# A transformer block and two differential-attention layers on one core: operand stacks assembled by DMA, fp32 value products in latent attention, and two squared sums moved into the gated output projection

## The reference

```python
s = jnp.einsum('bqhcd,bkhcd->bhcqk', qb, k) * scale
p = jax.nn.softmax(s, axis=-1)
a = p[:, :, 0] - lam_f * p[:, :, 1]
o = jnp.einsum('bhqk,bkhd->bqhd', a, vf)
```

## Time and profile before

| | us |
|---|---|
| median of 3 runs | 3114.75 (3114.37 to 3115.37) |
| the profiled execution, its own time | 3113.21 |
| its span in the profile | 3111.4 |
| TensorE matmul busy | 2752.8 (88%) |
| TensorE weight load busy | 2348.3 (75%) |
| VectorE busy | 1334.4 (43%) |
| ScalarE busy | 1004.3 (32%) |
| GpSimd busy | 526.2 (17%) |
| mean granted TensorE clock | 0.945 |
| DMA queue 1, share of 16 engines | 16.2% |

### The profile page before, as it was taken

One profiled execution on the slowest core, in us unless ns is written; L12 is line 12 of the kernel. 1 busy time (PEld: TensorE's weight loads), 2 busy tenths in 40 slices (PEclk: granted clock), 3 DMA queues, 4 the chain that ended last, 5 costly groups with the idle time before them and its releaser, 6 DMA issues. The chain is left out here.

```text
span 3111.4 us, 35654 instructions
## 1 busy us (share of the span) xinstructions
PE 2752.8 (88%) x14623; PEld 2348.3 (75%) x14623; DVE 1334.4 (43%) x1631; ACT 1004.3 (32%) x1538; POOL 526.2 (17%) x317
## 2 busy tenths in 40 slices
PE   4999677888879999999975999979997999978999
PEld 1877565787758888888855999768887998767877
DVE  4742753444453333333346212257743412227762
ACT  3312332544242111112213222157631322227640
POOL 0100121331000000000000000048720100008840
PEclk9999888999989999999987999989989999998989
DMA  5531001000211111111102123100022113210022
GB/s 210 176 122 46 14 7 48 14 1 1 95 39 42 49 53 47 47 47 47 48 28 82 50 63 92 48 8 1 1 96 85 68 38 82 52 44 1 1 82 81
DMA packets 58479, 167.92 MB, mean 54 GB/s; under 512 B 6368, under 2 KB 25184, under 8 KB 56672
## 3 DMA queue, kind: packets, MB, share of 16 engines
q1 hardware_dynamic: 58336, 165.92, 16.2%
HBM read 148.93 MB, written 16.97 MB: 53 GB/s over the span
## 5 line engine op out<-in xcount | busy, mean ns | idle before, releaser
L1810 DVE TENSOR_REDUCE da_negmax<-ps 128x1 f32<-128x1040 f32 x136 | 168.4, 1239 | 83.7 <-PE ps L1678 83.6
L1678 PE MATMUL ps<-st_k,st_q 128*128 128x264 f32 (+1 forms) x816 | 173.1, 352 | 35.0 <-DVE st_q L1919 26.5
L1709 PE MATMUL ps<-da_aT,v 128*128 128x128 f32 (+1 forms) x1224 | 161.0, 277 | 32.0 <-DVE da_aT L1736 27.3
L1709 PEld LDWEIGHTS ps<-da_aT,v 128*128 128x128 f32 x1224 | 146.9, 191 | 44.8 <-DVE da_aT L1736 34.9
L2141 DVE SCALAR_TENSOR_TENSOR res<-ps,gates,res 128x1024 f32<-128x1024 f32 x64 | 79.2, 1280 | 226.2 <-PE ps L2190 226.2
L1794 POOL TENSOR_TENSOR da_E<-da_E,da_F 128x1040 f32<-128x1040 f32 x68 | 163.9, 2411 | 5.7
L1678 PEld LDWEIGHTS ps<-st_k,st_q 128*128 128x128 f32 x816 | 125.4, 203 | 46.3 <-issue 27.4
L2104 ACT ACTIVATE ff_wh<-ff_raw 128x1024 fp32r<-128x1024 f32 x64 | 67.5, 1057 | 284.1 <-PE ps L2190 278.4
L2190 PE MATMUL ps<-ff_h_hi,ff_wh 128*128 128x512 f32 x512 | 157.8, 389 | 0.0
L2190 PE MATMUL ps<-ff_h_lo,ff_wh 128*128 128x512 f32 x512 | 157.7, 389 | 0.0
L2190 PE MATMUL ps<-ff_h_hi,ff_wl 128*128 128x512 f32 x512 | 157.7, 389 | 0.0
(11 more groups left out here) (433 smaller groups left out, 6464.6 us busy)
## 6 DMA issues: line engine op xcount, KB each, us to landing
ff_raw<-w_ff SPq DMA_DIRECT2D x64, 512.0 KB, 3.2
ada_w<-w_ada SPq DMA_DIRECT2D x16, 1024.0 KB, 7.5
wo_ring<-w_out SPq DMA_DIRECT2D x22, 512.0 KB, 4.3
residual_spill<-res SPq DMA_DIRECT2D x2, 4160.0 KB, 11.2
res<-xT SPq DMA_DIRECT2D x2, 4096.0 KB, 13.6
ada_w<-w_ada SPq DMA_DIRECT2D x4, 2048.0 KB, 26.8
pqk_raw<-w_in SPq DMA_DIRECT2D x16, 512.0 KB, 3.7
pg_raw<-w_in SPq DMA_DIRECT2D x16, 512.0 KB, 4.1
```

Source lines behind the costliest of these rows:

```text
L1678: mm = pe.matmul(k.ps[:, 3 * (n % 2) + b, a:a + w], q[:, qa:qa + P], kk[:, key:key + w], start=(j == 0), stop=(j == 1))
L1709: mm = pe.matmul(k.ps[:, 7, 0:w], v(g // NQ, t), aT[g % 2][:, t, 0:w], start=(t == 0), stop=(t == NT - 1))
L1810: dve.tensor_reduce(nm[:, n % 4:n % 4 + 1], window(n), AX.X, ALU.max, negate=True).then_inc(s_nm, 1)
```

## The change

Three parts, in neutral words.

1. `Stacks` is rewritten. ScalarE rounds the whole 128-partition key and query of a head (two copies), VectorE or GpSimd subtracts them in place (two subtractions, into the memory of `qk`), and eight DMAs of 64 partitions x 1040 issued from SP put the halves where they belong. The second pass of a component takes the query's rest straight from that memory, a contraction over 64 rows, so that lo·lo is no longer summed. For the first head this is done as the `side` of the value projection; for the others beside the head before, in blocks 0 to 2. The last query block of a head uses only its real rows as weights. `diff_attention`'s SP also loads the first weights of the output projection.
2. Latent attention gets its own function, `latent_heads`: values and transposed weights stay fp32, each batch of transposes is copied once (0 and 2 on ScalarE, 1 on VectorE), value products are one fp32 matmul of 128 columns per key tile and block, and three of the five score passes come ahead of the transposes of two blocks before, two behind.
3. In `GateTiles` the sums of heads 2 and 3 move from before the first product to steps 0 and 1; the turns move from steps 1 and 2 to 3 and 4, the spreads from step 3 on to step 5 on; the order of ScalarE's and VectorE's work around them changes with that.

The core of the diff (classes that only gain a base class with empty methods are left out, as is the removed `attention`):

```diff
-                    for t in key_tiles:
-                        vh, vl = v(g // NQ, t)
-                        for i, (a, b) in enumerate(((vh, ah), (vl, ah), (vh, al))):
-                            mm = pe.matmul(k.ps[:, 7, 0:w], a, b[:, t, 0:w], start=(t == 0 and i == 0), stop=(t == NT - 1 and i == 2))
...
+def latent_heads(nc, k, name, heads, NQ, splits, n_keys, v, scale, o_dst, e0, at0, then, then_at):
...
+    LAG, EARLY = 2, 3
...
+                def pv(g):
+                    pe.wait_ge(s_at1, g + 1)
+                    pe.wait_ge(s_at, 2 * g + 1)
+                    for t in range(NT):
+                        if t == 8:
+                            pe.wait_ge(s_at, 2 * g + 2)
+                        mm = pe.matmul(k.ps[:, 7, 0:P], v(g // NQ, t), aT[g % 2][:, t, :], start=(t == 0), stop=(t == NT - 1))
+                    mm.then_inc(s_pv, 1)
+
+                for g in range(NG + LAG):
+                    i = g - LAG
+                    if g < NG:
+                        scores(g, True)
+                    if i >= 0:
+                        turn(i, 0)
+                        turn(i, 1)
+                    if g < NG:
+                        scores(g, False)
+                    if i >= 0:
+                        turn(i, 2)
+                        pv(i)
...
+                for g in range(NG + LAG + 1):
+                    i = g - LAG
+                    if i >= 1:
+                        out(i - 1)
+                    if 0 <= i < NG:
+                        evacuate(act, i, 0, s_at)
+                    if 1 <= g <= NG:
+                        exps(g - 1)
+                    if 0 <= i < NG:
+                        evacuate(act, i, 2, s_at)
...
+class Stacks(Side):
+    banks = 8
+    PIECES = 8
...
+    def act(self, act, m):
+        if m in (3, 4):
+            self.round(act, 0, m - 3)
+    def dve(self, dve, m):
+        if m in (4, 5):
+            self.rest(dve, 0, m - 4)
+    def sp_last(self, sp):
+        self.copy(sp, 0)
+        sp.wait_ge(self.s_built, 16 * self.PIECES)
+    def round(self, act, h, x):
+        if h > self.head:
+            act.wait_ge(self.s_built, 16 * self.PIECES * (h - self.head))
+        src, dst = ((self.qk[:, AH + h, :], self.kh), (self.qk[:, h, :], self.qh))[x]
+        act.activation(dst[:], src, ACT.Copy).then_inc(self.s_hi, 1)
+    def copy(self, sp, h):
+        half = [slice(0, 64), slice(64, P)]
+        kk, q, low = self.k[h % 2], self.q[h % 2], self.low[:, AH + h, :]
+        if h >= 2:
+            sp.wait_ge(self.s_scores, (h - 1) * self.per_head)
+        done = 2 * (h - self.head)
+        sp.wait_ge(self.s_hi, done + 1)
+        for c in range(2):
+            sp.dma_start(kk[c][half[c], :].bitcast(F32), self.kh[half[c], :].bitcast(F32)).then_inc(self.s_built, 16)
+        sp.wait_ge(self.s_low, done + 1)
+        for c in range(2):
+            sp.dma_start(kk[c][half[1 - c], :].bitcast(F32), low[half[c], :].bitcast(F32)).then_inc(self.s_built, 16)
+        sp.wait_ge(self.s_hi, done + 2)
+        for c in range(2):
+            for r in range(2):
+                sp.dma_start(q[c][half[r], 0:L2].bitcast(F32), self.qh[half[c], :].bitcast(F32)).then_inc(self.s_built, 16)
+        sp.wait_ge(self.s_low, done + 2)
+    def passes(self, h, c, qa, w):
+        half = slice(64 * c, 64 * c + 64)
+        kk = self.k[h % 2][c]
+        return [(self.q[h % 2][c][:, qa:qa + w], kk), (self.low[half, h, qa:qa + w], kk[half, :])]
...
-                        if g // NQ + 1 < heads:
-                            for x in stacks.ACT_TURNS.get(g % NQ, ()):
-                                stacks.round(act, g // NQ + 1, x)
+                        if g // NQ + 1 < heads and g % NQ < 2:
+                            stacks.round(act, g // NQ + 1, g % NQ)
...
-                    if g // NQ + 1 < heads and g % NQ < stacks.REST_STEPS:
-                        if g:
-                            pool.wait_ge(s_A, g)
-                        stacks.rest(pool, g // NQ + 1, g % NQ)
-                        pool.wait_ge(stacks.s_rest, stacks.REST_STEPS * (g // NQ + 1) + g % NQ + 1)
+                    if g // NQ + 1 < heads and 1 <= g % NQ <= 2:
+                        stacks.rest(pool, g // NQ + 1, g % NQ - 1)
...
-        self.at_step = {1: [("turn", 0), ("turn", 1)], 2: [("turn", 2)] if len(self.batches) > 2 else []}
+        self.at_step = {0: [("sum", 2)], 1: [("sum", 3)], 3: [("turn", 0), ("turn", 1)], 4: [("turn", 2)] if len(self.batches) > 2 else []}
         for u in range(U):
-            self.at_step.setdefault(3 + u // 2, []).append(("spread", u))
+            self.at_step.setdefault(5 + u // 2, []).append(("spread", u))
...
     def ahead_pe(self, pe):
+        self.sum_of(pe, 0)
+        self.sum_of(pe, 1)
```

More of the change, by code:

```diff
@@ L254, in _, with open, sp_first, sp @@
                 ada.gains(dve, (0, 1))
-class AdaRest:
+class Side:
+    banks = 5
+    def open(self, freed=None):
+        pass
+    def sp_first(self, sp):
+        pass
+    def sp(self, sp, m):
+        pass
+    def sp_last(self, sp):
+        pass
+    def act(self, act, m):
+        pass
+    def dve(self, dve, m):
+        pass
+    def pe(self, pe, m, j=0):
+        pass
+    def pool(self, pool):
+        pass
+class AdaRest(Side):
     COLS, SLOTS = 256, 3
@@ L993, in gemm_tokens @@
         n_w = len(groups) * KT
-        NBK = 5 if side else 8
+        NBK = side.banks if side else 8
+        few = NBK < 8
         if side:
@@ L1010, in _ @@
                     fetch_first(sp, k, then)
+                if side:
+                    side.sp_last(sp)
             def evac(act, g):
@@ L1042, in _ @@
                        .then_inc(w_lo, 1)
-                    if split and n % KT == (0 if side else min(2, KT - 1)) and n >= KT:
+                    if split and n % KT == (0 if few else min(2, KT - 1)) and n >= KT:
                         lo(n // KT - 1)
@@ L1071, in _ @@
                     pe.sem_inc(summed, 1)
+            if side:
+                @block.gpsimd
+                def _(pool):
+                    side.pool(pool)
 def retention_tables(k, tab0):
@@ L1634, in diff_attention @@
-def diff_attention(nc, k, name, heads, NQ, q0, n_q, n_keys, v, o_dst, e_at, at_at, comp_w, stacks, first_sums):
+def diff_attention(nc, k, name, heads, NQ, q0, n_q, n_keys, v, o_dst, e_at, at_at, comp_w, stacks, first_sums, then, then_at):
     NT = -(-n_keys // P)
@@ L1662, in diff_attention, with _ @@
         s_T, s_at, s_at1, s_pv, s_o, s_z = (k.sem(f"{name}_{n}") for n in ("turned", "aT", "aT_middle", "pv", "o", "zeroed"))
-        stacks.open(s_S, NQ * 2, 0)
+        stacks.start("next", 1, s_S, NQ * 2)
         with nc.Block() as block:
+            @block.sync
+            def _(sp):
+                for h in range(1, heads):
+                    stacks.copy(sp, h)
+                fetch_first(sp, k, then, then_at)
             @block.tensor
@@ L1800, in _ @@
                 z.then_inc(s_z, 1)
-                for x in range(stacks.REST_STEPS):
-                    stacks.rest(dve, 0, x)
                 def maxes(g, c):
@@ L2774, in between @@
         for kind, u in self.at_step.get(step, ()):
-            if kind == "turn":
+            if kind == "sum":
+                self.sum_of(pe, u)
+            elif kind == "turn":
                 if u == 0:
```

527 lines of the change are left out of this document (168 added, 359 removed).

## The result

The changed kernel takes 3089.64 us (median of 4, 3087.42 to 3095.9) against 3115.06 for the kernel before (median of 4): a ratio of 0.9922, 95% interval 0.9904 to 0.9939. So it is 25 us faster, where 68 were forecast, and the time lies outside the forecast's range (3034 to 3064). The direction was right and the size was not. The profiled execution took 3091.63, with a span of 3089.9.

What follows compares the result with a forecast made beforehand. TensorE, busy 88% of the span, was taken as the bound. Terms -28 - 2 - 20.6 - 33.5 + 16.5 = -67.6 from 3113.2 gave 3045.6, or 3047 on the median's footing; range 3034 to 3064.

Steps and rivals of the forecast that it cites:

- Latent attention, -28 and -2: Latent attention: frames without waits, 6.17 a block against 6.86, -28 us; value projection without five subtractions, -2.
- The rival of frames at 6.6: Latent attention stays paced by waits, frames of 6.6, +13, giving 3061; chance 0.14.
- First head's stacks, -20.6: Start of differential attention, both layers: stacks ready beforehand, first scores 10.3 us earlier in each, -20.6.
- 6 to 12 us, hidden: First head's eight DMAs: time taken beside the value projection, within a 17.5 us window.
- The estimate of 10.9: First head's eight copies by the skill's rate for 64-partition halves: 10.9 us, still inside the window.
- Heads 1 to 3, -33.5: Differential attention, both layers: frames lengthened by GpSimd subtractions shrink towards 5.05, leaving 3 of 36 us excess, -33.5.
- GateTiles, +16.5: Output projection: moved sums now on the path, later spreads, stalls on `y_lo`; +10.5 first layer, +6 second.
- That the first product would not come forward: Output projection, first layer: moving two sums hardly brings the first product forward, since TensorE then waits for `y_lo`.
- The rivals: Latent waits stay (0.14); sums cost nothing (0.12); GpSimd goes on stalling (0.10); copies run one after another (0.04).
- that GpSimd goes on stalling: Differential attention: subtractions still stall 12 of 36 frames, leaving 12 to 15 us in place of 3, 3058; chance 0.10.

Runs made afterwards that it cites:

- the run with three more DMAs: Changed kernel plus three DMAs a head putting the query's rest into both halves, so every score product has 128 rows, whole computation kept: 3045.75 us.
- the half-height run: Changed kernel with the first score pass also cut to 64 rows, so all score products have 64 rows, key's rest left out: 3110.87 us.
- the run by pieces: Changed kernel with the same products reordered, 128-row then 64-row for each of three key pieces, 12 height changes a block instead of 4: 3221.58 us.

## Why the prediction failed

- **Latent attention, -28 and -2**: right. 25.6 and 3.9 by the trace, and the 4.0 behind it, for which the forecast had no term. The frame is 6.24 where 6.17 stood. The rival of frames at 6.6 did not happen.
- **First head's stacks, -20.6**: right, -19.3. Eight copies take 11.7, at the upper edge of the "6 to 12 us, hidden". The estimate of 10.9 from the Trainium skill (SBUF — State Buffer, "Door 1: The DMA port swizzle") was nearer than the middle of that range, and the trace agrees with it within 1 us.
- **Heads 1 to 3, -33.5**: the step that failed. Two statements are in it. That the GpSimd stalls go was right: with blocks of full height the stretches from the first scores to the last value product are 14.9 and 15.5 shorter than before (the run with three more DMAs), 30 in all. The failed one is the sentence "The product with the query's rest over 64 rows is costed as one over 128: what counts is the columns that pass." For a product by itself that holds (the half-height run). But the change of height between products does not come free: 0.18 to 0.195 us each, four in a block, 68 blocks, 50 us. It was a new shape in the middle of a stream of another shape; a range of nought to something was due for it, and none was given.

  The price could have been read beforehand. The differential attention of the kernel before has no such neighbourhood, but its gate projection has: two products of 16 rows stand between groups of twelve of 128 rows. Timeline of the kernel before:

```profile
1935.03 0.18 PEld L2551 LDWEIGHTS ps<-hn_rstd_hi,hn_spread 16*128 16x128 f32 x1 [0.22 <-issue]
1935.03 0.42 PE L2551 MATMUL ps<-hn_rstd_hi,hn_spread 16*128 16x348 f32 x1
...
1935.54 0.74 PE L943 MATMUL ps<-h_hi,pg_wh 128*128 128x348 f32 x3
1936.12 0.63 PE L943 MATMUL ps<-h_lo,pg_wh 128*128 128x348 f32 x3
1936.59 0.64 PE L943 MATMUL ps<-h_hi,pg_wh 128*128 128x348 f32 x3
...
1937.63 0.42 PE L2551 MATMUL ps<-hn_rstd_hi,hn_spread 16*128 16x346 f32 x1
```

The bracket is the same `issue`, and the load begins with its product. Three products of 128 rows behind each other take 0.47 (1936.12 to 1936.59). From one pair of 16-row products to the next it is 2.60 (1935.03 to 1937.63) for 14 products, which at 0.157 each would take 2.20: 0.4 too long for two changes, 0.2 each. At 0.2 the 272 changes of the attention are 54 us, and the sum would have come out near 3100.

The Trainium skill says it in one sentence, which was overlooked: "Changing tiling mode (not just tile) drains the TensorE" (TensorEngine Tiling (Array Packing), Key Properties). If a product of 64 rows is another tiling mode in its sense, the traces agree with it: the weight load that usually runs ahead begins with its product at each change. The page has no figure; these runs give 0.18 to 0.2 us at a granted clock of 1.
- **GateTiles, +16.5**: right in direction and close in size, +18.8 by the traces. That the first product would not come forward was right to a tenth. In the first layer one pair of traces gives 3.3 for the sums and 9.4 for the later spreads, where 5.5 and 5 were taken; if that split holds, two errors cancel in part, and the nearness of the total is partly luck. The stalls themselves are 2.1 and 1.6. What else there is goes with a lower clock behind them, for which the forecast had no term (windows of the changed kernel; granted clock third from the end; in the kernel before it is 1.00 from 2291 to 2321, after its own first products):

```profile
2273.00:2292.00 19.00, 15.39 (x53) 13.29 (x54) 8.71 (x12) 3.22 (x3) 0.00 (x0) 0.65 0.00 0
```
- **The rivals**: that GpSimd goes on stalling (12 to 15 left) had its mechanism in the traces, and a size of 7 (3.2 and 3.5 in the run with three more DMAs). `da_mixed` still takes 1.1 to 2.5 us in 14 of the 68 blocks of that run (the others from 0.22 on), but only two blocks a head have a subtraction. None of the rivals had a cost on TensorE's own side of the attention, though TensorE was named as the bound.

The ledger is then complete: -25.6 - 3.9 - 19.3 + 18.8 as foreseen or nearly so, -6.8 in phases that had no term, and in differential attention -30 from the builds, +50 from the changes of height, and about -4 that is left over. What it is made of was not tried; the intervals of the exponentials fit that longer blocks hide what remained of the stalls, and two blocks at the lower clock (8.85 and 9.04) work against that.

## What to carry to other kernels

When a change brings in a product of another shape, cost its neighbours, not only itself, and look through the whole trace, not only the phase that changes, for a place where such shapes already meet. On a kernel bound by TensorE, keep one contraction height through the inner loop, even at the price of copies or of useless rows; three DMAs off the critical path bought back 44 us here. Before moving work out from in front of a first instruction, ask what else that instruction waits for; if something else ends at the same time, the moved work only changes from hidden to exposed. And busy time cannot tell the difference between multiplying and changing over: compare the starts of like groups.

## What the runs showed of the hardware that was not expected

- A change between weights of 128 rows and of 64 rows costs 0.18 to 0.195 us at a granted clock of 1 (blocks of 5.05, 5.43, 5.78 and 7.34 with 0, 2, 4 and 12 changes), and one between 128 and 16 rows 0.2 (the kernel before).
- The granted clock fell in stretches in which TensorE is shown fully busy: to 0.68 in 2079 to 2099 of the half-height run (20.00 of 20 busy). The long blocks at the lower clock are found only in kernels with changes of height: one in each layer in the changed kernel, five in the half-height run, five of 12.7 us in the first layer of the run by pieces; the kernels of full height have no block over 6.7 us. The low clock at the start of the first layer's attention also lasts longer with them: until 12 to 18 us behind the first scores at full height, 22 to 27 with two or four changes a block, 30 in the half-height run, 39 by pieces. Whether the changes bring it about was not tried by itself.
- Eight DMAs of 64 partitions, 260 KB each, take 11.7 us from the first issue to the last landing beside a value projection.
